# Half-array products of two head chains, alternated head by head, in the time-mix tiles of a three-layer kernel

## What is computed

```python
RW_HEADS = 8
RW_HEAD_DIM = 64
...
    out = rwkv7_scan(time_major(both(r_h)), time_major(both(-kk)),
                     time_major(kk[:, :, None] * a_h), time_major(both(v_h)),
                     time_major(k_h), time_major(_heads(decay, H, N)))
    out = jnp.moveaxis(out, 0, 1)
    o = out[:, :, 0] + jnp.flip(out[:, :, 1], axis=1)
```

## Time and profile before

| | us |
|---|---|
| median of 3 runs | 3953.91 |
| lowest and highest of them | 3953.03, 3954.66 |
| the profiled execution | 3952.75 |
| its span from first to last instruction | 3951.0 |
| first tile's products start at | 2376.4 |
| last of the fourth tile's products starts at | 2750.3 |
| the four tiles together | 346.7 |
| mean granted clock of TensorE, as a share of 2.4 GHz | 0.927 |

### The profile page before, as it was taken

How to read it: one execution, slowest core, us unless ns; L and a number is a source line. 1 busy time by engine, 2 the same in 40 slices (tenths; PEclk the granted TensorE clock), 3 DMA queues, 4 the chain that set the end, 5 groups by cost and what they waited for, 6 DMA issues and landing times. The chain is left out here.

```text
span 3951.0 us, 59446 instructions
## 1 busy us (share of the span) xinstructions
PE 3479.3 (88%) x20672; PEld 2990.0 (76%) x20672; DVE 2460.4 (62%) x4973; ACT 1490.4 (38%) x2280; POOL 424.3 (11%) x460
## 2 busy tenths in 40 slices
PE   6878999999785979999999679788669799999996
PEld 5777899999763867999999637566338679999994
DVE  4688666666555797666666553434226976666663
ACT  4246444444342255444444321111222554444443
POOL 0165000000000373000000000000003730000000
PEclk8999999999898999999999887777789999999998
DMA  4411555555431303555555310000024135555552
GB/s 187 155 54 59 186 186 186 190 182 191 150 146 54 133 33 115 184 190 184 187 188 184 137 70 1 1 1 18 14 99 162 33 104 188 187 187 185 190 183 98
DMA packets 126707, 511.75 MB, mean 130 GB/s; under 512 B 14704, under 2 KB 15344, under 8 KB 119152
## 3 DMA queue, kind: packets, MB, share of 16 engines
q1 hardware_dynamic: 126576, 510.07, 36.4%
HBM read 508.96 MB, written 1.05 MB: 129 GB/s over the span
## 5 line engine op out<-in xcount | busy, mean ns | idle before, releaser
L406 PE MATMUL ps<-xh,uhigh 128*128 128x256 f32 x3072 | 870.3, 283 | 15.8 <-POOL ulow L788 15.8
L408 PE MATMUL ps<-xh,ulow 128*128 128x256 f32 x3072 | 869.2, 283 | 0.0
L407 PE MATMUL ps<-xl,uhigh 128*128 128x256 f32 x3072 | 869.1, 283 | 0.0
L406 PEld LDWEIGHTS ps<-xh,uhigh 128*128 128x128 f32 x3072 | 588.1, 191 | 33.8 <-POOL ulow L788 20.8
L407 PEld LDWEIGHTS ps<-xl,uhigh 128*128 128x128 f32 x3072 | 588.2, 191 | 13.0
L408 PEld LDWEIGHTS ps<-xh,ulow 128*128 128x128 f32 x3072 | 588.1, 191 | 0.0
L753 DVE TENSOR_TENSOR ulow<-stream,uhigh 128x1024 fp32r<-128x1024 f32 x330 | 404.3, 1225 | 183.4 <-ACT uhigh L531 183.4
L531 ACT CAST uhigh<-stream 128x1024 fp32r<-128x1024 f32 x336 | 352.9, 1050 | 414.9 <-DMA stream<-in_u 414.9
L424 PE MATMUL ps<-vhigh,chigh 128*128 128x512 f32 x1536 | 479.9, 394 | 2.7 <-DVE vlow L769 2.4
L758 DVE TENSOR_TENSOR stream<-stream,big 128x256 f32<-128x256 f32 x336 | 217.8, 648 | 422.7 <-ACT stream L589 422.6
L424 PE MATMUL ps<-vlow,chigh 128*128 128x512 f32 x1536 | 475.9, 391 | 0.0
(11 more groups left out here) (420 smaller groups left out, 4569.8 us busy)
## 6 DMA issues: line engine op xcount, KB each, us to landing
stream<-in_u SPq DMA_DIRECT2D x384, 512.0 KB, 4.2
stream<-in_v SPq DMA_DIRECT2D x369, 512.0 KB, 3.5
big<-in_wq SPq DMA_DIRECT2D x24, 1152.0 KB, 7.7
stream<-in_ab_w_in SPq DMA_DIRECT2D x4, 2048.0 KB, 11.3
stream<-in_c_w_qf SPq DMA_DIRECT2D x16, 512.0 KB, 3.5
stream<-in_c_w_ig SPq DMA_DIRECT2D x4, 2048.0 KB, 8.3
big<-in_w_gates SPq DMA_DIRECT2D x4, 2048.0 KB, 8.0
spare<-in_v SPq DMA_DIRECT2D x15, 512.0 KB, 3.5
```

The costliest lines, as they stand in the source:

```text
L406: pe.matmul(out, uh[:, b, cols], c.xh[:, k, :], start=k == 0, stop=False)
L407: pe.matmul(out, uh[:, b, cols], c.xl[:, k, :], start=False, stop=False)
L408: ins = pe.matmul(out, ul[:, b, cols], c.xh[:, k, :], start=False, stop=k == KD - 1)
```

## The change

`rwkv_tile` is written again. The same products are made, 464 MATMUL records for a tile as before, with another order and other banks:

- The list of steps is gone. Each engine has its own hand-written order, and semaphores of single purpose (`products`, `copied`, `added` and so on) stand in place of the three step counters.
- In every half-array product the loop runs over `heads`, which is (h, 0), (h, 1) for h = 0 to 3, so the two chains alternate head by head. This holds for the first block products, for the transposed product, for `QH`, `M`, `KV` and for the four chunks.
- `QH`, `M`, `KV` and the next-state product `M3` of both chains write into the same banks, chain 0 into partitions 0 to 63 and chain 1 into 64 to 127. So `qh`, `mt`, `kv` and the state are each read and written by one instruction over 128 partitions instead of two over 64.
- In a chunk all eight next-state products come first, with an increment of `mt_done`, and then all eight output products. Before, the two kinds alternated head by head.
- The `kt` by `ar` product is moved from s = 0 to behind the third growth of the inverse (`lk_done`).
- The expansions of `bh` (VectorE) and `vt` (ScalarE, four activations with a scale for each chain) and the copy of `at_` into `x` stand first in the tile. `mt`'s first part (`decayed_eye`) is made in two pieces between other VectorE work. `mt` moves into the free buffer of `k`.

```diff
-            for s in range(STEPS - 1):
-                for e in range(2):
-                    if s:
-                        pe.wait_ge(dve_done[e], s)
-                        pe.wait_ge(act_done[e], s)
-                    step(e, s).then_inc(pe_done[e], 1)
+            for h, e in heads:
+                r = rows_of(e)
+                ins = mm(wide(4 * e)[:, h, :], bt[r, h, tok], ar[r, h, :, tok])
+            ins.then_inc(lb_done, 1)
+            for h, e in heads:
+                r = rows_of(e)
+                ins = mm(quad(e, 2)[:, h], ar[r, h, 0, tok], bt[r, h, tok])
+            ins.then_inc(l1_done, 1)
...
+            for h, e in heads:
+                r = rows_of(e)
+                ins = mm(wide(4 * e)[:, h, :], kt[r, h, tok], ar[r, h, :, tok])
+            ins.then_inc(lk_done, 1)
...
+            for h, e in heads:
+                ins = mm(QH[rows_of(e), h], bufs[e]["ut"][:, h, RW_N:P], bufs[e]["lb"][:, h])
+            ins.then_inc(qh_done, 1)
+            for h, e in heads:
+                ins = mm(M[rows_of(e), h], bufs[e]["ut"][:, h, RW_N:P], bufs[e]["bm"][:, h * 256:(h + 1) * 256])
+            ins.then_inc(m_done, 1)
...
+            for h, e in heads:
+                mm(KV[rows_of(e), h], per_head(bh, e)[:, h], bufs[e]["um"][:, h * 256:(h + 1) * 256], stop=False)
+                ins = mm(KV[rows_of(e), h], per_head(kh, e)[:, h], bufs[e]["vm"][:, h * 256:(h + 1) * 256],
+                         start=False)
+            ins.then_inc(kv_done, 1)
+            pe.wait_ge(mt_ready, 3)
+            pe.wait_ge(qh_ready, 1)
+            for i in range(4):
+                n, x = order[i], i % 2
+                if i:
+                    pe.wait_ge(state_ready, i)
+                for h, e in heads:
+                    r = rows_of(e)
+                    ins = mm(M3[r, h], by_n(mt)[r, h, n, :], state[r, x, h, :])
+                ins.then_inc(mt_done, 1)
+                for h, e in heads:
+                    r = rows_of(e)
+                    ins = mm(O[32 * n:32 * n + 32, e, h], qh[r, h, 32 * n:32 * n + 32], state[r, x, h, :],
+                             start=False, stop=False, free=True)
+            ins.then_inc(o_done, 1)
...
+            for e in range(2):
+                split(bufs[e]["bm"], per_head(bh, e)).then_inc(splits_ready, 1)
+                ins = dve.tensor_copy(bufs[e]["x"][:, :, RW_N:P], per_head(at_, e))
+            ins.then_inc(splits_ready, 1)
...
+            for i in range(4):
+                dve.wait_ge(mt_done, i + 1)
+                dve.tensor_tensor(state[:, 1 - i % 2], M3, by_n(kv)[:, :, order[i], :], ALU.add).then_inc(state_ready, 1)
```

More of the change, by code:

```diff
@@ L1870, in rwkv_tile, with rows_of, by_head @@
+    heads = [(h, e) for h in range(H) for e in range(2)]
+    def rows_of(e):
+        return slice(RW_N * e, RW_N * e + RW_N)
+    def by_head(x):
+        return x.rearrange("p (h n) -> p h n", h=H)
     bufs = []
-    for e in range(2):
-        m = a if e else ring
-        lb = m.take(H * 256).rearrange("p (h two t) -> p h two t", h=H, two=2)
+    for m in (Arena(c.ring), a):
         lk = m.take(H * 256).rearrange("p (h two t) -> p h two t", h=H, two=2)
-        l1l1t = m.take(1024)
+        both_l = m.take(1024)
+        l1, l1t = by_head(both_l[:, 0:512]), by_head(both_l[:, 512:1024])
@@ L1876, in rwkv_tile @@
         pd = m.take(H * 256).rearrange("p (h two t) -> p h two t", h=H, two=2)
[L1877 to L1886, removed]
+        offt, l2, lb, x, z, ut = (m.tiles(H, P) for _ in range(6))
@@ L1905, in mm @@
                 return pe.matmul(out, lhsT, rhs, start=start, stop=stop, skip_group_check=free)
[L1907 to L1955, removed]
@@ L1964, in _ @@
+            ins.then_inc(o_done, 1)
         @block.scalar
         def _(act):
[L1966 to L1995, removed]
+            for e in range(2):
+                for n in range(4):
+                    ins = act.activation(by_n(bufs[e]["vm"])[:, :, n, :], per_head(vt, e), ACT.Copy,
+                                         scale=c.quarter[:, n:n + 1])
@@ new lines, in _, with grow @@
+            decayed_eye(0)
+            def grow(e, b):
+                p1 = bufs[e]["pd"][:, :, 1, :]
+                return dve.tensor_tensor(p1, p1, quad(e, b), ALU.add)
+            for e in range(2):
+                dve.wait_ge(products[e], 2)
+                grow(e, 1).then_inc(added[e], 1)
+            for e in range(2):
+                dve.wait_ge(products[e], 3)
+                grow(e, 2).then_inc(added[e], 1)
+            dve.wait_ge(lk_done, 1)
+            for e in range(2):
+                dve.tensor_tensor(bufs[e]["lk"].rearrange("p h two t -> p h (two t)"), wide(4 * e),
+                                  bc(both[:, dr, :], 1, H), ALU.mult).then_inc(lk_ready[e], 1)
```

213 lines of the change are left out of this document (146 added, 67 removed).

## The result

The changed kernel takes 3797.8 us (median of 4 runs, 3795.8 to 3801.5) against 3954.3 for the kernel before (4 runs, 3953.0 to 3956.3) on the same chip. The ratio is 0.9605, with a 95% interval of 0.959 to 0.962. The forecast was 3803, with a range from 3789 to 3836. The profiled execution has a span of 3797.4 us, 153.6 less than before.

The account below looks back on a forecast made before the run. TensorE was taken to bound the four tiles; 3.7 + 26.5 + 9.6 + 7.0 was given as 46.9 us a tile, taken as 49 for the clock, so 196 in place of 346.7 and 3803 us, range 3789 to 3836.

Parts of the forecast that it names:

- TensorE as the bound, four times over: In the four tiles TensorE sets the time, nothing hides it, and the kernel saves each tile's saving four times: 150.7 us.
- The tile's length: One tile takes 46.9 us at 2.4 GHz from the squaring on, taken as 49 with the clock, range 46 to 53.
- (a): Block products and masks at the tile's start: 3.7 us in place of 16.1.
- (b): From the transposed product through squaring, growth and solves, up to QH: 26.5 us in place of 29.35.
- (c): QH, M, output products and KV: 9.6 us in place of 18.35.
- (d): Four chunks and the tile's end: 7.0 us, or 9.1 at 1.2 GHz, in place of 22.7.
- the allowance of 2.1 us a tile: Tile's clock: late rise in the squaring loses 1.8 us, cold chunks 2.1; half of both, 46.9 taken to 49.
- Halves in turn run at about twice the pace: Half-array products alternating between halves overlap: in retention 0.232 us a record, against 0.357 in the old block products.
- Rival 2: Pairs sharing a bank don't overlap: M3 alone 3815, within the forecast's 0.78; with QH, M, KV 3839, 0.15 shared with rival 1.
- Rival 1: Issue bounds QH and chunks, 1.8 us per 16-record run: 58 us a tile, 3839; chance 0.15 with rival 2's full form.
- rival 3: No halves overlap in the tiles, the order saves only shorter waits: 72 us a tile, 3894; chance 0.04.
- Rival 4: Halves don't overlap and each of a tile's 112 turns drains the array: at 0.18 us a turn 3976; chance 0.02.

Follow-up runs that it names:

- e10: Changed kernel with half-array products chain after chain as in e1, TensorE also waiting for one chain's products to end before starting the other's; 3898.3 us.
- e3: Changed kernel with only the three row-half products ahead of the chunks (bt by ar, transposed, kt by ar) written chain after chain; 3806.2 us.
- e1: Changed kernel with all half-array products written chain after chain; 3825.2 us.
- e2: Changed kernel with only the products of the four chunks written chain after chain; 3806.4 us.
- e4: Changed kernel with only QH, M and KV written chain after chain; 3809.3 us.
- e7: Changed kernel with next-state and output products alternating again for each head in the chunks, chains still head by head; 3871.7 us.

## Why the prediction was right, and where its reason was too narrow

**TensorE as the bound, four times over: right.** 160.4 us went in the tiles, and the span gained no more than that.

**The tile's length: right within its bounds.** The sum at 2.4 GHz was 46.9 us and I took 49 for the clock; 47.5, 45.8, 47.1 and 45.9 came. Part by part in the first tile: the block products' masks begin 3.8 us after the start (3.7 in the sum), the squaring begins at 6.3 (6.15), `QH` at 31.1 (30.2), the chunks at 41.1 (39.9), and the chunks with the end take 6.4 (7.0). Term by term (a) was 0.1, (b) 0.7 and (c) 0.4 too short and (d) 0.6 too long. (The four terms add up to 46.8, not 46.9.)

**The clock: the allowance of 2.1 us a tile was the mis-sized term.** I split the odds between a clock that holds through the chunks and one that falls. It held in all four tiles, and it was up 5.5 us into the first tile and 3.7 into the third. In every tile of before and of e10 the row halves at its start began at 1.2 GHz and ended so; the rise came with the full-array products, 21 to 23 us into the tile in before and 16 to 19 in e10. That the overlap brings the clock is thus likely, but no run varies it alone, and e3 leaves a doubt: in its third tile the clock rose only 14.2 us after the tile's start, in its first 6.0, in e1's third 6.8, all with the same writing. What made that tile late was not found.

**The 7 us that came back elsewhere** cancelled most of that: the tiles gained 9.7 us more than forecast, the span only 2.9 more than the 150.7. That the time came so near the forecast is luck to that extent. The 7 us were not forecast; they lie in stages that did not change, some of them in their scatter.

**"Halves in turn run at about twice the pace": the step is right, and `M3` with them.** The two halves of `M3` share a bank and run together: 16 records of 64*64 start within 0.46 us (2423.37 to 2423.83 in the first tile), where those of one half alone start 0.058 apart (e2), 0.87 from the first to the last of sixteen. Rival 2 in its `M3` form did not come true. The Trainium skill, in TensorEngine Tiling (Array Packing), Gotcha 1, says that different row tiles cannot access one PSUM bank at the same time; here two row halves that write to different partitions of one bank did, with starts 0.006 us apart, and the measurement decides. Rival 1, a bound by issue that would cost 1.8 us for such a run, is refuted by the same row.

**What was too narrow is why the old order did not overlap.** I took the alternation in the program as the cause, and put e1 at 100 us on rival 3's figures. It cost 27. The halves also overlap when written chain after chain, since TensorE takes the other chain's products early (e4). What had kept the chains of before apart were three other things that the change also removes: runs of sixteen records of one half in step 0, longer than TensorE reaches past (e4); a wait between the two chains' runs (put back in e10: 100 us, of which I count some 80 as overlap); and, in the chunks, a change of form between any two products (put back in e7: 74 us, 71 of it in the tiles, though the chains are written in turn). The traces of before held the sign of it: in retention the loop writes two products of one half, four records, before it turns to the other half, and they ran at the paired pace; and 36 records of 256 columns would have taken 15.4 us at the 0.427 from start to start that they show alone, where 12.87 stood, so even before, some of chain 1's went beside chain 0's.

**Rival 3 was sized well**: 72 us a tile and 3894 for no overlap; e10 has 73.6 in the mean and 3898, with 4 to 7 us a tile of added waits in it. Rival 4, drained turns, has nothing for it in any run.

## What to carry to other kernels

Products that use half of the array need two things before the order of heads matters: no wait between the two halves' products, and one form in a row; then TensorE overlaps much by itself, as far as its reach of four records goes, and alternating them head by head adds the rest (27 us of 157 here). Look in the trace for pairs of records whose starts lie a few hundredths apart; where they are absent, ask which semaphore or which change of form stands between the halves. When a stage gets twice as fast, look at what the other engine does at its start: work that was hidden under it (here the expansions under the first products) can move ahead of what TensorE waits for next.

## What the runs showed of the hardware that I had not expected

- TensorE starts products of the other array half ahead of earlier ones in the program that wait for the first half, but only from four records away: in e4, after four records of chain 0 alone (0.46 us), the chains alternate though the program has eight of chain 0 first; in before, twelve of sixteen go alone.
- A change of form between any two products takes away all overlap of the halves: eight pairs of 64*64 and 64*32 in 6.0 us at 1.2 GHz, although the chains are written in turn (e7). Grouped and paired, two runs of 16 records take 1.21 us at 2.4.
- Two row halves may write to two partition halves of one bank at the same time without loss (`M3`).
- Short records are fed fast: 16 products and 16 weight loads in 0.61 us from start to start of two runs, 0.019 us for each of them.
